# Two-layer hybrid encoder: the high and low parts of the 16 meta rows in one weight-load operand

## The chip, the cores and the metric

The kernel runs on one core of a Trainium2 chip. The metric is the device time of one execution, in microseconds (us). The trace is that of one profiled execution. Engines are called PE (TensorE, matrix products), PEld (TensorE's weight loads), DVE (VectorE), ACT (ScalarE), POOL (GpSimd) and SP (SyncE, which here only issues transfers).

## What is computed

The input has 512 rows of 1024 numbers, and 16 learned meta rows are put ahead of them. All is float32. Cut to what matters here:

```python
h = concat([meta, x])                                        # 528 x 1024
h = h + short_conv_mixer(rmsnorm(h, a_norm), a_w_in, a_conv, a_w_out)
h = h + hier_moe(rmsnorm(h, ffn_norm[0]), ...)               # 32 experts, top 2 of a group
kv = rmsnorm(h, kv_norm) @ w_kv                              # K and V, of all 528 rows
k = partial_rotary(k)
h = h[16:]                                                   # the meta rows end here
h = h + diff_attention(rmsnorm(h, b_norm), w_q, ..., k, v)   # q @ w_q of 512 rows
h = h + hier_moe(rmsnorm(h, ffn_norm[1]), ...)
return rmsnorm(h, final_norm)
```

## The kernel before

**Tiles.** The rows lie in five tiles: t = 0 to 3 with 128 rows of the input each, and t = NX = 4 with the 16 meta rows. The second layer (attention and its experts) has only the four full tiles.

**Products in high and low parts.** The dense products outside the experts run in fp32r. To keep float32's precision, each operand is split in two: ACT casts it to fp32r (the high part, `act_high`, `weight_high`), and DVE subtracts this from the original (the low part, `act_low`, `weight_low`). The helper `product` then makes, for each of the KC = 8 chunks of the contraction, three matmuls into one PSUM bank: high rows with high weights, high rows with low weights, low rows with high weights. The rows are the operand that is loaded as weights (128 columns for a full tile, 16 for the meta tile), and 512 columns of the weight matrix are what streams through. So a job, one tile by 512 output columns, is 24 matmuls, whether it has 128 rows or 16.

**Where the meta tile has jobs.** In the mixer's output projection of the first layer, `out_proj(0, 4)`: two jobs one after the other, the last of five tiles. And among the 28 JOBS of the K, V and Q projections, in this order: K columns 0 to 511 for tiles 0 to 4 (jobs 0 to 4), K columns 512 to 1023 (5 to 9), V in the same way (10 to 19), Q for tiles 0 to 3 (20 to 27). Jobs 4, 9, 14 and 19 are the meta tile's. In all, six jobs of 24 matmuls.

**Order of the work around the mixer's projection.** PE runs tile by tile: the projection of t, the transposes of tile t - 1 (`turn`, L873), the router's logits of tile t - 2 (L935). DVE adds the projection to the stream h (`add_tile`, L1303), ACT takes the root mean square and scales the row, PE transposes it. After the last tile DVE runs the routing, POOL gathers the first rows (L594), and the first expert starts. When PE has finished the last tile's projection it gives four units of the weight ring back (`pe.sem_inc(unit_used, 4)`); SP waits for that before it issues the first large burst of expert weights: six transfers of 2 MB.

**Order of the work in the projections.** PE runs job p into PSUM bank 4 + p % 4; it waits for ACT's copy of job p - 4 out of that bank. ACT copies job p, scaled with the row's factor, to `knat` (K and Q) or to `V` (L813), and then casts the quarter of the next weight unit that stands at p in SPLIT_AFTER. DVE applies the rotary embedding to job p (`rotate`, L1496 to L1499), copies the transposed heads of the job before (`take_rot`, L1507), and makes the low part of the quarter (L1222). PE transposes the rotated rows (`turn_rot`, L1115) one job late. After each meta job PE waits for its own matmuls and gives two ring units back, for which SP loads the next of w_kv, w_q or b_w_out.

**The experts.** Each expert takes three weight units of 2 MB from the ring or from the arena, SP reissues them as PE frees them, and POOL gathers the rows of each expert and scatters the results with indirect transfers.

## Time and profile before

| | us |
|---|---|
| runs of the kernel | 1638.17, 1640.92, 1640.74 |
| their median | 1640.74 |
| the profiled execution | 1639.19 |
| its span, first to last instruction | 1637.4 |
| mean granted TensorE clock | 0.940 of full speed |
| PE busy | 1362.4 (83%) |
| DVE busy | 382.0 (23%) |
| ACT busy | 315.6 (19%) |
| POOL busy | 189.9 (12%) |
| moved by the DMA engines | 472.66 MB |

The line names are those of the kernel before. Matmuls are pipelined and the end of each is modelled, so the duration of one (about 395 ns with 512 columns) is longer than the distance between the starts of two. A row of the timeline merges neighbouring instructions of a line: start, duration of the whole, engine, line, operation, what it writes and reads, how often, and in brackets the idle time of the engine ahead of it and what ended that. In the windows the clock is a share of 2.4 GHz: 1.00 and 0.50 are the two levels.

### The profile page before, as it was taken

The page shows a single profiled execution, that of the slowest core. Times are in us where ns is not written, and L with a number is a line of the kernel's source. Part 1 is how long each engine was busy: PE and PEld are TensorE (multiplying, and loading weights), DVE is VectorE, ACT ScalarE, POOL GpSimd, SP SyncE. Part 2 cuts the span into 40 slices and gives each one's busy share as a digit, 9 for nine tenths or more (in the row PEclk, how much of TensorE's full clock was granted, in tenths as well). Part 3 has the DMA queues.
Part 4 walks back from the last instruction along what each step waited for, and adds up shares of the span by engine and source line. Part 5 has one row for each costly group of instructions (what it writes and reads, how often), then busy time and mean ns, then how long its engine had stood idle before and what let it go on. Part 6 is the DMA issues. An engine that isn't in the chain of part 4 may idle for free. (4 is left out here: it accounts for less than half of the span.)

```text
span 1637.4 us, 17518 instructions
## 1 busy us (share of the span) xinstructions
PE 1362.4 (83%) x6689; PEld 757.7 (46%) x6689; DVE 382.0 (23%) x753; ACT 315.6 (19%) x601; POOL 189.9 (12%) x314
## 2 busy tenths in 40 slices
PE   5999994999888888775999978895999888888882
PEld 5999772333322322223676755783333322322320
DVE  3434423000000000004531388623000000000003
ACT  5222220101000000003322266431010000000002
POOL 2000001111111111111000000001112111111111
PEclk9999995999999999997999979996999999999996
DMA  9120417999999999994312110417999999999994
GB/s 344 41 104 1 167 60 315 417 425 426 425 426 427 426 425 426 425 417 168 127 52 103 52 52 1 154 55 305 415 425 427 425 426 427 424 424 425 426 377 162
DMA packets 60921, 472.66 MB, mean 289 GB/s; under 512 B 10592, under 2 KB 10668, under 8 KB 35776
## 3 DMA queue, kind: packets, MB, share of 16 engines
q1 hardware_dynamic: 46480, 441.48, 65.2%
q0 software_dynamic: 14384, 30.36, 5.0%
q8 instruction: 42, 0.69, 0.2%
q14 instruction: 15, 0.12, 0.0%
HBM read 465.17 MB, written 23.13 MB: 298 GB/s over the span
## 5 line engine op out<-in xcount | busy, mean ns | idle before, releaser
L947 PE MATMUL ps<-ring,act 128*64 128x512 f32 x1792 | 442.0, 646 | 76.4 <-DMA ring<-in_e_up 70.3
L947 PEld LDWEIGHTS ps<-ring,act 128*64 128x64 f32 x1792 | 139.8, 142 | 373.8 <-issue 373.8
L914 PE MATMUL ps<-parts 128*128 128x512 f32 (+1 forms) x1104 | 266.0, 399 | 8.3 <-DVE parts L1230 7.7
L970 PE MATMUL ps<-ring,act 128*64 128x512 f32 x896 | 204.6, 597 | 31.0 <-ACT act L767 31.0
L1413 DVE TENSOR_TENSOR act<-act,ps 128x256 f32<-128x256 f32 x64 | 26.9, 421 | 869.6 <-ACT act L765 869.6
L914 PEld LDWEIGHTS ps<-parts 128*128 128x128 f32 (+1 forms) x1104 | 194.7, 178 | 69.3 <-DVE parts L1230 5.9
L900 PE MATMUL ps<-parts 128*128 128x264 f32 x1152 | 144.5, 288 | 4.5 <-DVE parts L1224 2.9
L900 PEld LDWEIGHTS ps<-parts 128*128 128x128 f32 x1152 | 143.1, 191 | 5.5 <-issue 5.5
L765 ACT ACTIVATE act<-ps 128x256 f32<-128x256 f32 x64 | 24.5, 383 | 573.8 <-PE ps L947 573.8
L970 PEld LDWEIGHTS ps<-ring,act 128*64 128x64 f32 x896 | 70.8, 136 | 126.2 <-issue 126.2
L607 POOL COPY dst_now<-dst_row 128x1 uint32 (+1 forms) x64 | 11.6, 181 | 686.8 <-ACT act L774 686.8
L774 ACT COPY act<-ps 128x512 f32<-128x512 f32 x64 | 37.4, 585 | 247.2 <-PE ps L970 247.2
L594 POOL DMA_INDIRECT nat<-hn_rows,src_now x64 | 66.9, 1045 | 57.2 <-POOL src_now L591 54.5
L610 POOL DMA_INDIRECT expert_rows<-act,dst_now x64 | 65.4, 1022 | 58.3 <-POOL dst_now L607 54.8
L956 PEld LDWEIGHTS ps<-const,nat 128*128 128x128 f32 x256 | 36.2, 210 | 68.6 <-issue 68.6
L947 PE MATMUL ps<-arena,act 128*64 128x512 f32 x256 | 63.1, 645 | 1.8 <-DVE act L1407 1.8
L697 ACT CAST parts<-ring 128x1024 fp32r<-128x1024 f32 x40 | 41.3, 1047 | 106.9 <-PE ps L900 106.7
L956 PE MATMUL ps<-const,nat 128*128 128x128 f32 x256 | 48.7, 313 | 15.5 <-DMA nat<-hn_rows,src_now 15.5
L1224 DVE TENSOR_TENSOR parts<-ring,parts 128x1024 fp32r<-128x1024 f32 x40 | 48.3, 1222 | 55.9 <-ACT parts L697 55.8
L962 PE MATMUL ps<-const,act 128*128 128x128 f32 x128 | 30.5, 320 | 23.4 <-DVE act L1413 23.4
L1407 DVE TENSOR_TENSOR act<-ps,block_gain 128x512 f32<-128x512 f32 x64 | 43.7, 683 | 14.9 <-PE ps L956 14.9
L660 ACT ACTIVATE nat<-h 128x1024 f32<-128x1024 f32 (+1 forms) x23 | 24.3, 1055 | 109.6 <-DVE h L1303 90.7
(164 smaller groups left out, 915.8 us busy)
## 6 DMA issues: line engine op xcount, KB each, us to landing
ring<-in_e_gate SPq DMA_DIRECT2D x56, 2048.0 KB, 18.3
ring<-in_e_up SPq DMA_DIRECT2D x56, 2048.0 KB, 22.6
ring<-in_e_down SPq DMA_DIRECT2D x56, 2048.0 KB, 22.3
arena<-in_e_down SPq DMA_DIRECT2D x8, 2048.0 KB, 15.8
ring<-in_a_w_in SPq DMA_DIRECT2D x6, 2048.0 KB, 19.6
arena<-in_e_up SPq DMA_DIRECT2D x6, 2048.0 KB, 19.2
arena<-in_e_gate SPq DMA_DIRECT2D x6, 2048.0 KB, 14.2
ring<-in_w_kv SPq DMA_DIRECT2D x4, 2048.0 KB, 13.4
```

The lines of the kernel that those rows point to most:

```text
L594: pool.indirect_dma_start(nat[:, b, 0:DH], None, hn_halves[layer], bass.IndirectOffsetOnAxis(src_now[:, b:b + 1], 0), bounds_check=2 * (LE ...
L610: pool.indirect_dma_start(y_halves[layer], bass.IndirectOffsetOnAxis(dst_now[:, u:u + 1], 0), y_out[:, u, :], None, bounds_check=4 * SPREA ...
L697: last = nc.scalar.copy(high, src)
L774: nc.scalar.copy(y_out[:, u, :], ps[:, 6 + u, :]).then_inc(y_ready, 1)
L900: last = mm(ps[:, b + a, 0:HALF], w[:, k, :], acts[:, k, a * HALF:(a + 1) * HALF], start=(k == 0 and i == 0), stop=(k == KC - 1 and i == 2))
L914: last = mm(bank, x[:, k, :], w[:, k, :], start=(k == 0 and i == 0), stop=(k == KC - 1 and i == 2))
L947: last = mm(ps[f * C:(f + 1) * C, 2 + b, :].rearrange("p (g m i) -> p g m i", g=2, i=2), x, w, start=(k == 0), stop=(k == KC - 1))
L956: last = nc.tensor.transpose(ps[:, b, c * P:(c + 1) * P], nat[:, b, c:DH:KC // 2], ident)
L962: last = nc.tensor.transpose(ps[:, 4 + b, c * P:(c + 1) * P], hidden[:, b, c:FE // 2:2], ident)
L970: last = mm(ps[o * C:(o + 1) * C, 6 + b, :], hT[:, b, (2 * c + a) * C:(2 * c + a + 1) * C], w[:, f * D + o * DH:f * D + (o + 1) * DH], sta ...
L1224: last = v.tensor_tensor(low, src, high, ALU.subtract)
L1407: return v.tensor_tensor(xT[:, b, :].rearrange("p (c a n) -> p c a n", **shape), ps[:, b, :].rearrange("p (c a n) -> p c a n", **shape), b ...
```

## The change

A tile `packed` holds, for each of the 8 chunks, 48 columns: the high part of the 16 meta rows, the high part again, and the low part. ACT's cast writes both copies of the high part in one instruction (its source is broadcast), and DVE writes the low part to columns 32 to 47.

For a meta tile `meta_product` takes the place of `product`: per chunk one matmul with all 48 columns against the high weights, and one with the first 16 columns against the low weights. So 16 matmuls in place of 24. The wide one writes 48 PSUM partitions: 0 to 15 get high by high (and, accumulated, high by low from the narrow one), 16 to 31 get a copy that nobody reads, 32 to 47 get low by high.

What lies in partitions 32 to 47 has to be added, and DVE does it: in the mixer's projection with one `tensor_tensor` more ahead of the old one in `add_tile`, each over 16 x 1024; in the projections with `add_meta(p)` for the four meta jobs, a `scalar_tensor_tensor` over 16 x 512 from PSUM, scaled with the row's factor, onto what ACT has copied to `knat` or `V`. It waits for ACT's copy, stands ahead of `rotate(p)` on DVE, and DVE waits for its end. PE waits for it before job p + 4 uses the bank again, and before attention.

```diff
+LOW_AT = 32
+        packed = sb("packed", [P, KC, LOW_AT + META], F32R)
...
+        META_JOBS = [p for p, j in enumerate(JOBS) if j[2] == NX]
...
+            if t == NX and group in (1, 2):
+                high, low = packed[:, :, 0:META], packed[:, :, LOW_AT:]
...
+                if t == NX and group in (1, 2):
+                    src, high = bcast(src, 2, 2), packed[:, :, 0:LOW_AT].rearrange("p k (a n) -> p k a n", a=2)
                 nc.scalar.copy(high, src).then_inc(act_high_ready, 1)
...
+            def meta_product(bank, n):
+
+                w_low, w_high = (chunks(ring_parts[m % RING][:, :]) for m in (n, n + 1))
+                for k in range(KC):
+                    if k:
+                        mm(ps[0:META, bank, :], packed[:, k, 0:META], w_low[:, k, :], start=False, stop=False)
+                    last = mm(ps[0:LOW_AT + META, bank, :], packed[:, k, :], w_high[:, k, :], start=(k == 0), stop=(k == KC - 1))
+                    if not k:
+                        mm(ps[0:META, bank, :], packed[:, k, 0:META], w_low[:, k, :], start=False, stop=False)
+                return last
...
+                if p - 4 in META_JOBS:
+                    pe.wait_ge(meta_added, META_JOBS.index(p - 4) + 1)
...
             pe.wait_ge(proj_copied, len(JOBS))
+            pe.wait_ge(meta_added, len(META_JOBS))
...
                     dve.wait_ge(out_done, (NX + 1) * layer + t + 1)
+                    if t == NX:
+                        order(v.tensor_tensor(h[0:r, t, :], h[0:r, t, :], flat[LOW_AT:LOW_AT + r, b * W:(b + 2) * W], ALU.add))
                     v.tensor_tensor(h[0:r, t, :], h[0:r, t, :], flat[0:r, b * W:(b + 2) * W], ALU.add).then_inc(mixed, 1)
...
+            def add_meta(p):
+
+                kind, f, _ = JOBS[p]
+                dst = V[0:META, NX, f * W:(f + 1) * W] if kind == "v" else knat[0:META, ROT_JOBS.index(p) % 2, :]
+                dve.wait_ge(proj_copied, p + 1)
+                v.scalar_tensor_tensor(dst, ps[LOW_AT:LOW_AT + META, 4 + p % 4, :], rstd[0:META, NX:NX + 1], dst,
+                                       ALU.mult, ALU.add).then_inc(meta_added, 1)
+                dve.wait_ge(meta_added, META_JOBS.index(p) + 1)
+
             for p in range(len(JOBS)):
+                if p in META_JOBS:
+                    add_meta(p)
```

`out_proj` and `project` call `meta_product` where t == NX, and `product` as before elsewhere.

On PE, around the meta job 9 of the projections, the instructions of the kernel before stand in this order (the last number of a row is the columns that stream, the one before it the columns of the operand that is loaded):

```order
L1115 MATMUL ps<-const,knat 128x128 x3
L914 MATMUL ps<-parts 16x512 [waits proj_copied]
L914 MATMUL ps<-parts 16x512 x23
L1115 MATMUL ps<-const,knat 128x128 [waits proj_done,rot_copied,roped]
L1115 MATMUL ps<-const,knat 128x128 x3
```

And with the change, at the same place:

```order
L1135 MATMUL ps<-const,knat 128x128 x3
L920 MATMUL ps<-parts,packed 48x512 [waits proj_copied]
L922 MATMUL ps<-parts,packed 16x512
L919 MATMUL ps<-parts,packed 16x512
L920 MATMUL ps<-parts,packed 48x512
L919 MATMUL ps<-parts,packed 16x512
L920 MATMUL ps<-parts,packed 48x512
```

The rows go on in pairs of a narrow and a wide matmul, up to 8 of each; what stands ahead of the job and behind it is as it was.

On DVE, at the end of the mixer's projection of the first layer, the kernel before has the add of tile 3, the transposed tile 2, and then the meta tile's add:

```order
L1303 TENSOR_TENSOR h<-h,ps 128x1024 [waits out_done]
L1213 TENSOR_TENSOR act<-ps,gain 128x8x128 [waits turned1]
L1208 RECIPROCAL rstd<-ssq 128x1 [waits squared]
L1303 TENSOR_TENSOR h<-h,ps 16x1024 [waits out_done]
L1213 TENSOR_TENSOR act<-ps,gain 128x8x128 [waits turned1]
L1208 RECIPROCAL rstd<-ssq 16x1 [waits squared]
```

With the change:

```order
L1326 TENSOR_TENSOR h<-h,ps 128x1024 [waits out_done]
L1234 TENSOR_TENSOR act<-ps,gain 128x8x128 [waits turned1]
L1229 RECIPROCAL rstd<-ssq 128x1 [waits squared]
L1325 TENSOR_TENSOR h<-h,ps 16x1024 [waits out_done]
L1326 TENSOR_TENSOR h<-h,ps 16x1024 [waits dve_step]
L1234 TENSOR_TENSOR act<-ps,gain 128x8x128 [waits turned1]
```

Two adds in a row stand where one stood, the second behind a wait for the first.

On DVE in the projections, at job 4, the kernel before has:

```order
L1507 COPY arena<-ps 128x4x128 [waits rot_turned]
L1222 SCALAR_TENSOR_TENSOR parts<-ring,gain,parts 128x512 [waits w_high_ready]
L1222 SCALAR_TENSOR_TENSOR parts<-ring,gain,parts 128x512
L1496 TENSOR_TENSOR rope<-knat,const 16x128 [waits roped,proj_copied]
L1497 TENSOR_TENSOR rope<-knat,const 16x8x8 [waits dve_step]
```

With the change:

```order
L1530 COPY arena<-ps 128x4x128 [waits rot_turned]
L1243 SCALAR_TENSOR_TENSOR parts<-ring,gain,parts 128x512 [waits w_high_ready]
L1243 SCALAR_TENSOR_TENSOR parts<-ring,gain,parts 128x512
L1537 SCALAR_TENSOR_TENSOR knat<-ps,rstd,knat 16x512 [waits proj_copied]
L1519 TENSOR_TENSOR rope<-knat,const 16x128 [waits roped,proj_copied,meta_added]
```

The added row is `add_meta(4)`, ahead of the rotation of the meta rows.

## Rows read from the trace of the kernel before

**Rows 1.** The page, part 2: 40 slices of 40.9 us; granted clock and DMA, tenths.

```profile
PEclk9999995999999999997999979996999999999996
DMA  9120417999999999994312110417999999999994
```

**Rows 2.** Groups of instructions by form: busy us, mean ns, idle before.

```profile
L914 PE MATMUL ps<-parts 128*128 128x512 f32 x960 | 232.0, 400 | 8.3 <-DVE parts L1230 7.7 <-PE ps L914 0.6
...
L914 PE MATMUL ps<-parts 128*16 128x512 f32 x144 | 34.3, 395 | 0.0
```

**Rows 3.** Timeline, PE: first tiles of the mixer's projection; in the projections jobs 4, 11 to 14, 15 to 19.

```profile
177.09 25.09 PE L914 MATMUL ps<-parts 128*128 128x512 f32 x96 [3.20 <-DVE parts L1230]
...
798.18 0.66 PE L1115 MATMUL ps<-const,knat 128*128 128x128 f32 x4 [2.67 <-DVE knat L1499]
798.59 5.81 PE L914 MATMUL ps<-parts 128*16 128x512 f32 x24
...
841.79 22.50 PE L914 MATMUL ps<-parts 128*128 128x512 f32 x96
864.60 28.02 PE L914 MATMUL ps<-parts 128*128 128x512 f32 x120 [0.30 <-PE ps L914]
```

**Rows 4.** Timeline, ACT's copies of jobs 13 and 14.

```profile
858.78 0.69 ACT L813 ACTIVATE arena<-ps,rstd 128x512 f32<-128x512 f32 x1 [3.65 <-PE ps L914]
...
864.33 0.68 ACT L813 ACTIVATE arena<-ps,rstd 16x512 f32<-16x512 f32 x1 [3.64 <-PE ps L914]
```

**Rows 5.** Timeline, PE: mixer's projection of tiles 3 and 4, meta transposes, first expert's rows.

```profile
216.75 11.36 PE L914 MATMUL ps<-parts 128*128 128x512 f32 x48
...
230.62 11.29 PE L914 MATMUL ps<-parts 128*16 128x512 f32 x48
...
246.08 1.13 PE L873 MATMUL ps<-const,nat 16*128 16x16 f32 x8 [0.95 <-ACT nat L680]
...
275.47 1.10 PE L956 MATMUL ps<-const,nat 128*128 128x128 f32 x4 [9.32 <-DMA nat<-hn_rows,src_now]
```

**Rows 6.** Timeline, DVE: the meta tile's add in the mixer's projection.

```profile
241.95 1.21 DVE L1303 TENSOR_TENSOR h<-h,ps 16x1024 f32<-16x1024 f32 x1 [10.86 <-PE ps L914]
```

**Rows 7.** Timeline of SP's issues: the first of the weight burst, and w_q.

```profile
242.03 0.33 SPq L454 DMA_DIRECT2D arena<-in_e_gate  x1
...
835.15 29.81 SPq L427 DMA_DIRECT2D ring<-in_b_w_q  x2
```

**Rows 8.** Timeline, POOL: the first gather of each layer.

```profile
268.80 1.12 POOL L594 DMA_INDIRECT nat<-hn_rows,src_now  x1 [0.96 <-POOL src_now L591]
...
1129.22 1.12 POOL L594 DMA_INDIRECT nat<-hn_rows,src_now  x1 [0.93 <-POOL src_now L591]
```

**Rows 9.** Timeline, PE behind the second layer's first gather.

```profile
1132.61 1.10 PE L956 MATMUL ps<-const,nat 128*128 128x128 f32 x4 [6.19 <-DMA nat<-hn_rows,src_now]
```

**Rows 10.** Windows: length, busy PE, PEld, DVE, ACT, POOL, then clock, DMA share, GB/s.

```profile
273.00:274.00 1.00, 0.00 (x0) 0.00 (x0) 0.00 (x0) 0.00 (x0) 0.00 (x0) 0.50 0.82 312
...
1129.00:1130.00 1.00, 0.00 (x0) 0.00 (x0) 0.00 (x0) 0.00 (x0) 0.78 (x1) 0.50 0.68 279
```

**Rows 11.** Transfers of the whole run: count, KB each, median us from issue to landing.

```profile
ring<-in_b_w_q SPq DMA_DIRECT2D x2, 2048.0 KB, 8.7
...
nat<-hn_rows,src_now POOLq DMA_INDIRECT x64, 8.9
```

**Rows 12.** Timeline, DVE around the end of job 4.

```profile
801.61 1.41 DVE L1222 SCALAR_TENSOR_TENSOR parts<-ring,gain,parts 128x512 fp32r<-128x512 f32 x2
805.14 0.28 DVE L1496 TENSOR_TENSOR rope<-knat,const 16x128 f32<-16x128 f32 x1 [2.13 <-ACT knat L813]
...
806.16 0.67 DVE L1507 COPY arena<-ps 128x512 f32<-128x512 f32 x1
```

**Rows 13.** Windows (columns as in rows 10): a change of the clock, and the projections.

```profile
182.00:183.00 1.00, 1.00 (x4) 0.80 (x3) 0.71 (x1) 0.00 (x0) 0.00 (x0) 0.61 0.88 377
...
800.00:940.00 140.00, 138.48 (x621) 102.86 (x620) 45.12 (x105) 35.35 (x55) 0.00 (x0) 1.00 0.22 76
```

More of the change, by code:

```diff
@@ L276, in build @@
         combined = [sem(f"combined{l}") for l in range(2)]
-        proj_done, proj_copied = sem("proj_done"), sem("proj_copied")
+        proj_done, proj_copied, meta_added = sem("proj_done"), sem("proj_copied"), sem("meta_added")
         roped, rot_turned, rot_copied = sem("roped"), sem("rot_turned"), sem("rot_copied")
@@ L926, in out_proj @@
                 for f in range(2):
-                    last = product(ps[0:r, b + f, :], high, low, n + 2 * f, (S_AOUT, S_BOUT)[layer] + f * QUARTERS if t == 0 else None)
+                    last = meta_product(b + f, n + 2 * f) if t == NX else product(ps[0:r, b + f, :], high, low, n + 2 * f, (S_AOUT, S_BOUT)[layer] + f * QUARTERS if t == 0 else None)
                 last.then_inc(out_done, 1)
@@ L1100, in project @@
                 _, high, low = act_tile(T_KVQ + t)
-                last = product(ps[0:r, 4 + p % 4, :], high, low, U_KVQ + 2 * u, S_KVQ + u * QUARTERS if t == 0 else None)
+                last = meta_product(4 + p % 4, U_KVQ + 2 * u) if t == NX else product(ps[0:r, 4 + p % 4, :], high, low, U_KVQ + 2 * u, S_KVQ + u * QUARTERS if t == 0 else None)
                 last.then_inc(proj_done, 1)
```

## The prediction

> **What bounds the kernel now.** Begin with the slices [rows 1]. In slices 8 to 18 and again in most of 28 to 38 the DMA engines are at 9 tenths: there the experts' weights stream, and the time of these stages is bytes over bandwidth, whatever PE does. The change touches neither; it can only move their start. What it touches lies in slice 5 (the mixer's projection of the first layer) and in slices 19 to 22 (the K, V and Q projections), where DMA is at 0 to 4 tenths. So the questions are whether PE sets the pace in these two places, and what stands behind each.
>
> The groups by form give the size [rows 2]: 144 matmuls with 16 loaded columns, 34.3 us busy, with no idle time ahead of them. Their mean of 395 ns is not what one costs, since neighbours overlap. The cost is the distance of starts. Jobs 15 to 19 are 120 matmuls in 28.02 us [rows 3]: (28.02 - 0.395) / 119 = 0.232 us each. One of these five jobs is the meta tile's. Alone, ACT's copies of jobs 13 and 14 follow each other by 5.55 us, which is the meta job 14: 5.55 / 24 = 0.231 us [rows 4]. In the mixer the meta tile's 48 take 11.29 us, the 128 rows' 48 take 11.36 us [rows 5]: (11.29 - 0.395) / 47 = 0.232. So a matmul costs 0.232 us with 16 and with 128 loaded columns alike, and a wide one of 48, which lies between, is priced at 0.232 too.
>
> In the projections PE is the pace: from 800 to 940 us it is busy for 138.48 of 140 us [rows 13], and its longest wait in the stage's jobs is the 2.67 us ahead of job 4, for DVE's rotation [rows 3]. In the mixer's projection PE runs from tile to tile as well; the meta tile is last, and DVE (10.86 us idle) waits for it [rows 6].
>
> **Part 1, the matmuls of the projections.** Four meta jobs lose 8 matmuls each: 32 x 0.232 = 7.4 us, all on PE's path. A new thing is the alternation of 48 and 16 columns, 64 times in these jobs, which no row shows. A border from 128 to 16 columns without anything between is that of jobs 13 and 14, and it shows in neither distance [rows 4]. For a bound from the other side take job 4 by itself, (5.81 - 0.395) / 23 = 0.235 us [rows 3]: 0.003 us more, over 96 matmuls in both stages 0.3 us. I take nothing, and see no reason for a gain.
>
> The Trainium skill, "TensorE: Matmul & The Clock Gate", section "Back-to-back issue gap", gives about 216 ns between matmuls of 512 columns at the full clock, and 131 ns in a sustained stream of weight loads and matmuls. By these the 48 removed matmuls would be worth 10.4 or 6.3 us instead of 11.1. The trace has 232 ns in just this stream, and the sum goes by the trace.
>
> **Part 2, what comes due earlier in the projections.** Every meta job ends 1.86 us sooner. What must be ready then?
> DVE, at job 4: the low part of the fourth quarter of the next weights ends at 803.02 [rows 12]. Job 5 would start at about 802.85 + 0.4, and needs that quarter only for its last two chunks, 18 x 0.232 = 4.2 us later. The first job after each meta job is covered by some 4 us.
> `add_meta(4)`: no row has this instruction. Its neighbours are one 512 column low part (half of 1.41, 0.70 us), a copy from PSUM (0.67 us) [rows 12], and half of the 16 x 1024 add (0.61 us) [rows 6]; I take 0.7, between 0.6 and 0.75. It starts when ACT's copy is there, near 803.3, and ends at 804.0; the rotation (1.0 us, from 805.14 to 806.16 in [rows 12]) ends at 805.0. PE asks for it behind job 5, near 808.9. Cover 3.8 us. What queues behind it on DVE is the rotation and the copy of the heads; before, DVE stood idle for 2.13 us there [rows 12], and the 1.86 us of job 4 and the 0.7 us use it up nearly. At jobs 14 and 19 there is no rotation, and only the add.
> PE's new wait at jobs 8, 13, 18 and 23 looks at an add four jobs old: nothing.
> ACT's cast writes 256 numbers a partition in place of 128; by its copy of 512 in 0.68 us [rows 4] that is at most 0.2 us. In the mixer it runs under tile 3's 11.36 us [rows 5]; ahead of job 4 it is in the stretch where ACT and DVE prepare jobs, so at most 0.2 us could reach the path. I take 0.
> SP: ring units come back earlier, so transfers shift with the jobs. For w_q the issue is at 835.15 [rows 7] and it takes 8.7 us [rows 11]; its first quarter is cast behind job 15, after 864.33 + 5.5 us. Over 20 us of cover.
> Projections: 7.4 us, from 7.1 to 7.5.
>
> **Part 3, the mixer's projection.** PE ends the meta tile 16 x 0.232 = 3.71 us sooner, at 238.2. Two things hang on this end.
> First, SP's weight burst: its first issue stands at 242.03 [rows 7], right behind PE. It moves by the full 3.71 us.
> Second, the chain to the router: DVE now adds twice. The new add is like the old, 1.21 us [rows 6], and one waits for the other, by estimate 0.03 us: 1.24 us. ACT, PE's meta transposes (246.08, rows 5), the logits, the routing on DVE and the gather on POOL move by 3.71 - 1.24 = 2.47 us.
> Both meet in the first gather. POOL issues it at 268.80 [rows 8], and PE starts on it at 275.47 [rows 5]: 6.6 us. In the second layer it took from 1129.22 to 1132.61 [rows 8, 9], 3.4 us. The difference is the burst. In the first layer the DMA engines are busy until about 273.9 (the window from 273 has 0.82), 5.1 us into the gather; in the second they are just running dry (0.68 at 1129) [rows 10]. Under full load a gather takes 8.9 us in the median [rows 11]. So under load it goes ahead at 3.4 / 8.9 = 0.38 of its free pace: 5.1 x 0.38 = 1.9 us of its work is done when the burst ends, 1.5 remain, 275.4. This fits the trace. It then moves with 0.62 of the burst's shift and 0.38 of its own: 0.62 x 3.71 + 0.38 x 2.47 = 3.2 us.
> Bounds: if the gather simply came behind the burst, 3.7 us; if only its issue counted, 2.5 us; if it were as free as in the second layer, it would land at 266.3 + 3.4 = 269.7, 5.6 us sooner. I take 3.2.
>
> The Trainium skill, "DMA: Bandwidth & Descriptors", section "Queues, rings and completion order", says that each DMA engine takes turns between the queues that have work. That speaks for the shared pace and against the strict "behind the burst": by it 3.2 us, by the other 3.7 us.
>
> The experts' stage then starts 3.2 us sooner and keeps its length, since its weights stream at full bandwidth from the first release on; its end and everything after moves along.
>
> **The sum.** 3.2 + 7.4 = 10.6 us. Against the profiled execution, 1639.19 - 10.6 = 1628.6. The median of the runs before is 1.55 us above the profiled execution, and the mean of the four executions is 1639.8; from it the time is 1629.2, which I give. About 3.3 us, 0.2%, is what a measurement can tell from no change.
>
> **Rivals.**
> The projections' gain is filled up again: the shorter meta jobs uncover DVE, as ahead of job 4 already (2.67 us). For it: 0.7 us more on DVE at each. Against it: the covers of 3.8 to 4 us. If all four lose their 1.86 us, 3.2 us remain: 1636.6.
> The mixer's gain is lost: PE's first expert starts as before, from something in the routing that I don't see. 7.4 us remain: 1632.4. For it only that the gather's landing is modelled.
> The gather is freed altogether: 5.6 + 7.4 = 13.0, 1626.8. Against it: the burst is still running for 3.9 us of it.
> The change doesn't do what it says: a matmul that writes 48 partitions costs as much as two of 16. Then 16 cost what 24 did, and the added add is left: +1.24 x 0.38 = 0.5 us, 1640.3. Against it: 128 columns cost 0.232 us.
> Slower: the granted clock. Its price is in the first 96 matmuls of the mixer's projection: 25.09 us where 96 take 22.50 later [rows 3], and the clock stands at the low level until within the window from 182 [rows 13], 5.4 us: PE loses half of the time spent at the low level. The place would be the projections: if fewer busy columns, 16 or 48 in the meta jobs, and PE's waits let the clock fall to 1.2 GHz, more than 10.6 / 0.5 = 21 us at the low level turn the gain into a loss. From job 4 to job 11 are 43 us [rows 3]; run low they would cost 21.6: 1629.2 + 21.6 = 1650.8. Against it: from 800 to 940 the clock is at 1.00 through all four meta jobs [rows 13], which were narrower then.
>
> **Chances.** Forecast 0.80, with a range of its own from 1626 to 1632; mixer's gain lost 0.05; gather freed 0.05; projections filled up 0.04; no effect 0.03; clock 0.03. The unknown costs make the gain 9.4 to 13.0 us, and single executions differ by about 1.4 us to each side. The range from 1625.0 to 1633.5 takes in the first three cases. Faster by over 0.2%: 0.80 + 0.05 + 0.05 + 0.03 of the filled case = 0.93. Within 0.2%: 0.04. Slower: 0.03.
>
> **What would show each step.** In the profile after: 96 matmuls for six meta jobs, copies of ACT around job 14 apart by 16 x 0.232 = 3.7 us. The burst's first issue near 238.3; DVE's two adds of 1.2 us; the first gather issued near 266.3 and PE on it near 272.2. Job 0 of the projections 3.2 us earlier, attention 10.6 us earlier, both experts' stages as long as before, and no wait of PE on DVE behind jobs 5 and 10. Copies of 5 us or more around job 14 would make part 1 wrong; PE at 273.0 with the gather issued at 266.3 the model of the gather; a clock of 0.50 between 800 and 930 the case of the clock.

## The result, and the profile after

| | before | after |
|---|---|---|
| median | 1639.45 us (1637.59 to 1640.92, 4 runs) | 1625.8 us (1624.37 to 1629.28, 4 runs) |
| profiled execution | 1639.19 us | 1626.44 us, span 1624.7 us |
| matmuls on PE | 6689 | 6641 |
| DVE instructions | 753 | 758 |

The ratio is 0.9915, interval 0.9898 to 0.9931: 13.7 us less, where 10.6 were forecast. 1629.2 us was given with a range from 1625.0 to 1633.5. The time lies in the range, 3.4 us under the forecast. The experiments below put the change itself at about 11 us, and the other 2.6 us at differences between executions of the same kernel.

The page of the kernel after, its slices of the granted clock and of the DMA engines, to be held against [rows 1]:

```profile
PEclk9999995999999999997999979996999999999996
DMA  9130427999999999995312200427999999999984
```

The experts' stages are again full of DMA, and no slice of the clock stands lower than before. The changes are too small for a slice and must be looked for in the timeline.

The groups of PE's matmuls by form (out<-in, tile, count, busy us, mean ns, idle before), against [rows 2]:

```profile
L932 PE MATMUL ps<-parts 128*128 128x512 f32 x960 | 231.4, 399 | 8.3 <-DVE parts L1251 7.7 <-PE ps L920 0.6
L920 PE MATMUL ps<-parts,packed 128*48 128x512 f32 x48 | 19.5, 409 | 0.0
```

The 144 narrow matmuls have become 48 wide ones (128*48) and 48 narrow ones. The wide one's mean of 409 ns against 395 of the old narrow one is no price: busy times of neighbours overlap, and some of these matmuls ran at the low clock (below).

The timeline of PE in the mixer's projection, against [rows 3, 5]: first 96 matmuls, the first wide one of the meta tile, the meta transposes, the first expert's rows.

```profile
176.18 24.04 PE L932 MATMUL ps<-parts 128*128 128x512 f32 x96 [3.20 <-DVE parts L1251]
...
228.64 0.41 PE L920 MATMUL ps<-parts,packed 128*48 128x512 f32 x1
...
241.63 1.14 PE L880 MATMUL ps<-const,nat 16*128 16x16 f32 x8 [2.20 <-ACT nat L685]
...
269.90 1.10 PE L974 MATMUL ps<-const,nat 128*128 128x128 f32 x4 [7.77 <-DMA nat<-hn_rows,src_now]
```

The same stretch on DVE, SP and POOL, against [rows 6 to 8]:

```profile
236.25 1.21 DVE L1325 TENSOR_TENSOR h<-h,ps 16x1024 f32<-16x1024 f32 x1 [7.14 <-PE ps L920]
237.50 1.21 DVE L1326 TENSOR_TENSOR h<-h,ps 16x1024 f32<-16x1024 f32 x1
```

```profile
236.34 0.33 SPq L459 DMA_DIRECT2D arena<-in_e_gate  x1
```

```profile
264.78 1.12 POOL L599 DMA_INDIRECT nat<-hn_rows,src_now  x1 [0.95 <-POOL src_now L596]
```

These have to be read against a zero point. The projection already starts 0.91 us sooner, and its first 96 matmuls take 24.04 us instead of 25.09, with the same instructions. The matmuls behind them start at 202.90 before and at 200.92 after: 1.98 us that lie ahead of everything the change touches. Taking them off:

| event | before | after | difference | less 1.98 | forecast |
|---|---|---|---|---|---|
| first issue of the weight burst | 242.03 | 236.34 | 5.69 | 3.71 | 3.71 |
| meta transposes | 246.08 | 241.63 | 4.45 | 2.47 | 2.47 |
| first gather issued | 268.80 | 264.78 | 4.02 | 2.04 | 2.47 |
| PE on the gathered rows | 275.47 | 269.90 | 5.57 | 3.59 | 3.2 |

The two adds of DVE take 1.21 us each and start 1.25 us apart (1.24 forecast), and the transposes move exactly as forecast. The gather is *issued* 0.43 us less early than forecast: the logits took 4.70 us instead of 4.29, since the granted clock fell to 0.50 as they began (in the window from 242, they start at 242.70), and before it fell within them (in the window from 247, they start at 247.14). And yet PE starts 0.4 us *earlier* than the model of the gather gave. This is the first thing to be settled.

In the projections, PE at job 3, ahead of job 4, ahead of job 5 and in it, and the 96 matmuls behind job 14, against [rows 3]:

```profile
782.73 5.82 PE L932 MATMUL ps<-parts 128*128 128x512 f32 x24
...
792.14 1.12 PE L1135 MATMUL ps<-const,knat 128*128 128x128 f32 x4 [2.56 <-DVE knat L1522]
...
798.22 0.63 PE L1135 MATMUL ps<-const,knat 128*128 128x128 f32 x4 [0.30 <-PE ps L920]
798.60 5.81 PE L932 MATMUL ps<-parts 128*128 128x512 f32 x24
...
854.35 22.48 PE L932 MATMUL ps<-parts 128*128 128x512 f32 x96 [0.30 <-PE ps L920]
```

ACT's copies of jobs 13 and 14, against [rows 4]:

```profile
850.39 0.69 ACT L820 ACTIVATE arena<-ps,rstd 128x512 f32<-128x512 f32 x1 [3.65 <-PE ps L932]
...
854.08 0.68 ACT L820 ACTIVATE arena<-ps,rstd 16x512 f32<-16x512 f32 x1 [1.78 <-PE ps L920]
```

The copies lie 3.69 us apart instead of 5.55, so job 14 lost 1.86 us: 8 x 0.232, as forecast. Job 9 lost 1.87 and job 19 lost 1.83. Behind jobs 4, 9 and 14 PE waits for nothing but its own last matmul (0.30 us). But at job 4 it is less. From job 3's start to job 5's are 15.87 us (782.73 to 798.60), and before it is 16.31 us, from these two rows of PE before:

```profile
788.77 5.82 PE L914 MATMUL ps<-parts 128*128 128x512 f32 x24
...
805.08 5.81 PE L914 MATMUL ps<-parts 128*128 128x512 f32 x24
```

That is 0.44 us less where 1.86 were forecast. The windows of the kernel after (columns as in [rows 10]) say why:

```profile
791.00:792.00 1.00, 0.00 (x0) 0.00 (x0) 0.90 (x6) 1.00 (x2) 0.00 (x0) 0.89 0.00 0
792.00:793.00 1.00, 0.86 (x5) 0.87 (x5) 1.00 (x3) 0.77 (x2) 0.00 (x0) 0.50 0.00 0
793.00:794.00 1.00, 1.00 (x5) 0.42 (x4) 1.00 (x3) 0.00 (x0) 0.00 (x0) 0.50 0.00 0
...
795.00:796.00 1.00, 1.00 (x5) 0.42 (x4) 1.00 (x3) 0.00 (x0) 0.00 (x0) 0.90 0.00 0
```

PE had stood idle for 2.56 us ahead of this job, waiting for the rotation on DVE, and the granted clock went from 1.00 to 0.50 (from 2.4 to 1.2 GHz) there and came back within the window from 795. The matmuls in it start 0.43 us apart instead of 0.232. Three microseconds at half speed are the 1.42 us that are missing. That is the mechanism of the rival "the granted clock", in small. Is it the change's doing? This is the second thing.

The third is the size of the whole: 13.7 us in the medians, 12.75 in the two traces, and not 10.6. At the end of the projections the two traces stand 12.07 us apart. Of it 5.57 are there at the first expert's rows (1.98 of them ahead of the change) and 5.56 at jobs 9, 14 and 19, 0.44 at job 4; the rest, some 0.5 us, are small differences of both signs between the stages. From there through attention to the end of its output projection both take 161.18 us.

### The profile page after: what moved, and what is told of

It is laid out like the page before. It is cut to its first block and busy times, and to the rows that moved or that the text cites. A ratio compares the mean times of both kernels' runs of the same rounds, so it can differ in the third digit from the quotient of the medians.

```text
span 1624.7 us, 17432 instructions
## 1 busy us (share of the span) xinstructions
PE 1348.6 (83%) x6641; PEld 753.7 (46%) x6641; DVE 386.4 (24%) x758; ACT 315.6 (19%) x601; POOL 190.3 (12%) x314
## 5 line engine op out<-in xcount | busy, mean ns | idle before, releaser
L932 PE MATMUL ps<-parts 128*128 128x512 f32 x960 | 231.4, 399 | 8.3 <-DVE parts L1251 7.7
L932 PEld LDWEIGHTS ps<-parts 128*128 128x128 f32 x960 | 180.8, 190 | 50.4 <-DVE parts L1251 5.9
L907 PEld LDWEIGHTS ps<-parts 128*128 128x128 f32 x1152 | 142.2, 190 | 5.5 <-issue 5.5
L974 PE MATMUL ps<-const,nat 128*128 128x128 f32 x256 | 48.7, 314 | 13.7 <-DMA nat<-hn_rows,src_now 13.7
## 6 DMA issues: line engine op xcount, KB each, us to landing
ring<-in_e_down SPq DMA_DIRECT2D x56, 2048.0 KB, 22.5
```

The lines of the kernel that those rows point to most:

```text
L907: last = mm(ps[:, b + a, 0:HALF], w[:, k, :], acts[:, k, a * HALF:(a + 1) * HALF], start=(k == 0 and i == 0), stop=(k == KC - 1 and i == 2))
L932: last = mm(bank, x[:, k, :], w[:, k, :], start=(k == 0 and i == 0), stop=(k == KC - 1 and i == 2))
L974: last = nc.tensor.transpose(ps[:, b, c * P:(c + 1) * P], nat[:, b, c:DH:KC // 2], ident)
```

## Experiments 1: each half alone, and the matmuls put back

Theory: 7.4 us come from four meta jobs of the projections and 3.2 to 3.7 from the mixer's meta tile, and both come from the 8 matmuls of 24 that a job loses. The rival says that something else in the change (the packed operand, the other order of operands, shifted transfers) brings a part.

The changed kernel again, as the base of this series, unaltered.

> The changed kernel once more, for a second trace and a tighter interval. Sum of the parts (32 matmuls of 0.232 us in the projections, 3.2 to 3.7 us through the mixer): 10.6 to 11.1 us less than the kernel before, ratio 0.9933. Rival, that something beyond these parts is systematic: the first comparison's 13.7 us again, ratio 0.9915. In the trace: 6 meta jobs of 16 matmuls, each 1.86 us shorter; the stretch up to the mixer's projection as in the kernel before but for the moment at which the clock rises.

The packed operand only in the mixer (group 1); the projections as before, without `add_meta`:

```
-            if t == NX and group in (1, 2):
+            if t == NX and group == 1:
                 high, low = packed[:, :, 0:META], packed[:, :, LOW_AT:]
...
-                last = meta_product(4 + p % 4, U_KVQ + 2 * u) if t == NX else product(
+                last = product(
...
-        META_JOBS = [p for p, j in enumerate(JOBS) if j[2] == NX]
+        META_JOBS = []
```

> Only the mixer's projection of the meta tile uses the packed operand (32 matmuls in place of 48, two adds on DVE); the projections of K and V have 24 matmuls a meta job and no add_meta. The sum of the parts: 3.2 us less than before if the gather shares the DMA engines with the weight burst, 3.7 us if it lands behind the burst's end; ratio 0.9979. Rival, that more comes from this place (gather freed as in the second layer): 5.6 us, ratio 0.9966.

Only in the projections (group 2); the mixer as before:

```
-            if t == NX and group in (1, 2):
+            if t == NX and group == 2:
...
-                    last = meta_product(b + f, n + 2 * f) if t == NX else product(
+                    last = product(
...
-                    if t == NX:
-                        order(v.tensor_tensor(h[0:r, t, :], h[0:r, t, :], flat[LOW_AT:LOW_AT + r, b * W:(b + 2) * W], ALU.add))
```

> Only the four meta jobs of the K and V projections use the packed operand; the mixer's projection is as before. All on PE's path: 32 x 0.232 = 7.4 us less, ratio 0.9955, at most 1.1 us of it lost where the clock is low in job 4. Rival, that DVE's added 0.74 us per job fills the gap: PE waits on DVE behind jobs 5 and 10, 0 to 3 us less.

Everything as in the changed kernel, but each narrow matmul issued twice, so that a job has 24 again:

```
-                    if k:
+                    for _ in range(2 if k else 0):
                         mm(ps[0:META, bank, :], packed[:, k, 0:META], w_low[:, k, :], start=False, stop=False)
...
-                    if not k:
+                    for _ in range(0 if k else 2):
```

> The changed kernel with its packed operand, its adds and its waits, but each chunk of a meta job has one narrow matmul more (high by low is made and counted twice, so this part of the meta rows' sum is wrong), 24 matmuls a job as before. If the gain is PE's matmuls alone, nothing is left of it: the added adds cost 1.24 us ahead of the router and are covered in the projections, 0 to 1.2 us more than before, ratio 1.0000 to 1.0008. Rival, that part of the gain comes from elsewhere (other operand, other placement of tiles, shorter weight loads): 2 to 3 us less than before, ratio 0.9985.

Measured, in five rounds beside the kernel before (median 1639.52 us, 1635.0 to 1643.6, 23 runs):

| kernel | median (range, runs) | ratio to before | gain |
|---|---|---|---|
| changed, again | 1629.74 (1626.55 to 1630.67, 6) | 0.9933 [0.9919, 0.9948] | 11.0 us |
| mixer only | 1635.66 (1631.35 to 1640.03, 12) | 0.9973 [0.9962, 0.9984] | 4.4 us |
| projections only | 1632.9 (1631.38 to 1636.17, 6) | 0.9954 [0.9938, 0.9970] | 7.5 us |
| 24 matmuls again | 1638.36 (1634.88 to 1643.21, 12) | 0.9992 [0.9979, 1.0006] | 1.3 us |

Three things follow. The gain is that of the removed matmuls: with them put back, at 48 and 16 columns, what remains is a ratio of 0.9992. Its interval takes in 1, but also the 0.9985 of the rival by which 2 to 3 us come from elsewhere, so the time alone does not settle it. The trace does, in the projections. ACT's copies of jobs 13 and 14 in this kernel:

```profile
862.22 0.69 ACT L820 ACTIVATE arena<-ps,rstd 128x512 f32<-128x512 f32 x1 [3.65 <-PE ps L932]
867.78 0.68 ACT L820 ACTIVATE arena<-ps,rstd 16x512 f32<-16x512 f32 x1 [3.65 <-PE ps L920]
```

They are 5.56 us apart, as in the kernel before (5.55), where 16 matmuls have 3.69. So the number of matmuls carries it, and the alternation of wide and narrow ones costs 0.01 us in a job. The two parts are 7.5 and 4.4 us; with the ratio's interval the first stands within 4.9 to 10.2 us and the second within 2.6 to 6.2. Both agree with 7.4 and with 3.2 or 3.7 for the mixer, and can't tell these two apart. And the changed kernel itself gains 11.0 us in this series, not 13.7; the two intervals overlap.

The kernel with the doubled matmuls shows what 16 of them cost in the path of the mixer's end: its burst is issued at 242.71 and PE is on the first rows at 275.81, where the changed kernel of the same series has 236.49 and 270.10. Its first 96 matmuls end 2.48 us later (202.84 and 200.36); this taken off, the burst moves by 3.74 us, 16 x 0.232 = 3.71, and the rows by 3.2.

## Experiments 2: does the first gather go by its issue, or by the burst?

The prediction let the gather go ahead at 0.38 of its free pace under the burst's load, so that it moves with 0.62 of the burst's shift and 0.38 of its own. The rival: its rows land behind the burst, however early it is issued. Two kernels pull the two apart.

The burst later: SP waits until DVE has added the meta tile; the chain to the gather is left as it is.

```
                 sp.wait_ge(unit_used, U_MOE[layer])
+                if layer == 0:
+                    sp.wait_ge(mixed, NX + 1)
```

> The changed kernel, but SP waits for DVE's last add of the mixer's projection before it issues the first layer's weight burst, 2.45 us later than PE's end. POOL's gather is issued as before. Behind the burst: PE's first expert starts 33.5 us after the burst's first issue as in the six traces so far, so 2.45 us later against PE's end than in the changed kernel, and the gather takes 7.6 us. Shared pace: 0.62 of 2.45, 1.5 us later. Issue alone: no difference.

The gather's issue earlier: the added add of the low part is left out.

```
-                    if t == NX:
-                        order(v.tensor_tensor(h[0:r, t, :], h[0:r, t, :], flat[LOW_AT:LOW_AT + r, b * W:(b + 2) * W], ALU.add))
```

> The changed kernel without the added add on DVE in the mixer's projection (the low part of the meta rows is not added to the stream in the first layer). The chain to the router is 1.24 us shorter, and the gather is issued that much sooner. Behind the burst: PE's first expert starts no sooner, 33.5 us after the burst's first issue, the gather takes 6.4 us. Shared pace: 0.5 us sooner. Issue alone: 1.24 us sooner.

The first kernel took 1633.56 us and the second 1630.31, in a single execution each. Such a time can't tell a microsecond. What counts is the distances inside each trace. SP's first issue, POOL's gather and PE's first rows, burst later:

```profile
241.10 0.33 SPq L459 DMA_DIRECT2D arena<-in_e_gate  x1
```

```profile
267.07 1.12 POOL L601 DMA_INDIRECT nat<-hn_rows,src_now  x1 [0.95 <-POOL src_now L598]
```

```profile
274.31 1.10 PE L976 MATMUL ps<-const,nat 128*128 128x128 f32 x4 [9.89 <-DMA nat<-hn_rows,src_now]
```

And one add only, POOL and PE (its burst is issued at 238.18):

```profile
264.67 1.12 POOL L599 DMA_INDIRECT nat<-hn_rows,src_now  x1 [0.95 <-POOL src_now L596]
```

```profile
272.17 1.10 PE L974 MATMUL ps<-const,nat 128*128 128x128 f32 x4 [10.14 <-DMA nat<-hn_rows,src_now]
```

All traces side by side but the two with an earlier burst, which follow below. E is the end of the first 96 matmuls of the mixer's projection, B the burst's first issue, G the gather's, S PE's start on its rows. The last two rows belong to the third series, below:

| kernel | G - B | S - G | S - B | S - E |
|---|---|---|---|---|
| before | 26.77 | 6.67 | 33.44 | 73.29 |
| before, again | 27.19 | 6.14 | 33.33 | 73.17 |
| projections only | 26.59 | 6.58 | 33.17 | 73.02 |
| changed | 28.44 | 5.12 | 33.56 | 69.68 |
| changed, again (first series) | 28.43 | 5.18 | 33.61 | 69.74 |
| mixer only | 28.44 | 5.46 | 33.90 | 70.03 |
| 24 matmuls again | 28.44 | 4.66 | 33.10 | 72.97 |
| burst later | 25.97 | 7.24 | 33.21 | 71.80 |
| one add only | 26.49 | 7.50 | 33.99 | 70.11 |
| changed, again (third series) | 28.44 | 5.20 | 33.64 | 69.77 |
| job 4 ahead | 28.42 | 5.17 | 33.59 | 69.72 |

G - B varies by 2.47 us, from 25.97 to 28.44. By the shared pace S - B should vary with it. The five short ones (before twice, projections only, burst later, one add only) have a mean G - B of 26.60 us, the six others of 28.44; 0.38 of the difference is 0.70 us. Instead their means of S - B, 33.43 and 33.57, differ by 0.14 us, with a scatter of 0.3 to 0.6 us to each side. A straight line through the eleven points has a slope of 0.07, with a 95% interval from -0.14 to 0.28: neither the 0.38 of the shared pace nor the 1 of "only its issue" lies in it. The time from the gather's issue, S - G, is what gives, from 4.66 to 7.50 us.

The two kernels made for this question, counted from E, against 69.7 in four traces of the changed kernel's mixer: with the burst 2.47 us later S comes 2.1 later, where "behind the burst" asks for 2.5, the shared pace for 1.5 and "only its issue" for nothing. With one add the gather is issued 1.95 us sooner (1.2 of it the add, the rest logits that ran at the upper clock), and S comes 0.4 us later, where the three ask for 0, 0.7 sooner and 1.95 sooner. So the rival fits best: in the first layer the rows are there some 33.5 us behind the burst's first issue, and the gather's own issue counts for little or nothing. The scatter of some half a microsecond that none of the models gives is not traced, and a share of the issue below 0.28 is not excluded.

The kernel before was run once more in this series, to see how much of the differences lies in the execution.

> The kernel before, for a second trace of it. Two readings of the clock ahead of job 4 of the projections, where PE stands idle for 2.6 us: in four of four traces of the changed kernel and its variants, and in the variant that has the old projections too, it fell to the low level there, in the first trace of the kernel before it did not. If the fall is a matter of the execution, it is as likely to fall here too. If it comes with the change, it doesn't fall. The gather: behind the burst, PE's first expert 33.5 us after the burst's first issue.

It took 1642.17 us, span 1640.3. In the mixer the first 96 matmuls took 22.52 us where [rows 3] have 25.09, and its burst was issued at 238.95 and not at 242.03 [rows 7]: 3.1 us sooner, and still its span was 2.9 us longer in the whole. So single places of one kernel differ by 2 to 3 us from execution to execution, as much as the 1.98 us that had to be taken off above. In this place it is the granted clock. The same 96 matmuls in this trace and in that of the changed kernel of the third series:

```profile
176.59 22.52 PE L914 MATMUL ps<-parts 128*128 128x512 f32 x96 [3.20 <-DVE parts L1230]
```

```profile
177.29 25.33 PE L932 MATMUL ps<-parts 128*128 128x512 f32 x96 [3.20 <-DVE parts L1251]
```

In each of the thirteen traces PE waits 3.20 us ahead of them. In two (this one and the early burst's, below) the clock stayed at 1.00 and they took 22.5 us; in five it fell and was back by the window from 181, 23.8 to 24.1 us; in six it was back only in the windows from 182 or 183, 25.1 to 25.4 us. The changed kernel is in both of the latter groups. So 1.05 of the 1.98 us above are a shorter fall of the clock, and not the change. The other 0.91 lie in the start of the 96 matmuls, which in three traces of the changed kernel itself stands at 176.18, 176.30 and 177.29. At job 4 the trace of before, again, shows this, PE:

```profile
796.64 1.12 PE L1115 MATMUL ps<-const,knat 128*128 128x128 f32 x4 [2.66 <-DVE knat L1499]
797.40 6.85 PE L914 MATMUL ps<-parts 128*16 128x512 f32 x24
```

The idle time of 2.66 us is as long as in [rows 3] (2.67), but the old job of 24 takes 6.85 us where it took 5.81: here the clock fell in the kernel before too. Of the traces with this idle time (2.55 to 2.67 us) it did not fall in the first one of before and in "one add only", and it fell in the nine others. It fell within the wait or up to 1.5 us behind it. How long it stayed at the low level differs: some 3 us in the changed kernel's first trace, nearly 7 in the second.

What this costs can be read from job 3's start to job 5's. Five of the traces:

| kernel | clock | job 3 to job 5 |
|---|---|---|
| before | stays up | 16.31 |
| before, again | low for some 3 us | 17.72 |
| one add only (job 4 as in the changed kernel) | stays up | 14.45 |
| changed | low for some 3 us | 15.87 |
| changed, again (first series) | low for nearly 7 us | 17.25 |

At the upper level in both, the change is worth 16.31 - 14.45 = 1.86 us at job 4 too, exactly 8 x 0.232. A fall costs 1.4 us in either kernel, the long one 2.8. So the fall goes with the wait ahead of job 4, which both kernels have, and it came with the old job of 24 matmuls too.

## Experiments 3: the burst earlier, and the wait ahead of job 4 taken away

Both findings name something that can be had. If the gather lands behind the burst, the burst should begin sooner. Ring slots of the first half of the last tile's weights are free once its half f = 0 is multiplied, and the first two transfers of the burst can go there. This stands in both layers. For it the last matmul of that half signals `half_done`, two loads wait on it instead of on the last unit, and DVE adds the two halves apart:

```
-        out_done = sem("out_done")
+        out_done, half_done = sem("out_done"), sem("half_done")
...
+                    if f == 0 and t == (NX if layer == 0 else NX - 1):
+                        last.then_inc(half_done, 1)
...
+                load(1, 0, "down", "half")
+                load(2, 1, "gate", "half")
                 sp.wait_ge(unit_used, U_MOE[layer])
...
-                load(1, 0, "down", None)
-                for part in ORDER:
+                for part in ORDER[1:]:
                     load(2, 1, part, None)
```

> The changed kernel with two additions: SP issues the two transfers whose ring units the first half of the last tile's projection frees already behind that half (1.86 us sooner in the first layer, 5.6 us in the second), and DVE adds each half of the last tile on its own, so that only the second half's adds stand behind PE's end (1.2 us less). Behind the burst: first expert 1.9 us sooner in the first layer, and by the shorter add 0.6 us in the second, 2.5 us less than the changed kernel, ratio to the kernel before 0.9918. Rival, that the burst isn't what the gather waits for: 1.2 us in the first layer and 0.6 in the second, ratio 0.9922; or that the transfers which the experts need first now come later: 0 or slower than the changed kernel.

It was timed in the second series, five rounds: 1625.88 us (1623.07 to 1626.58, 5 runs) beside 1639.39 of before, ratio 0.9910 [0.9895, 0.9926]. SP, POOL and PE:

```profile
231.64 0.33 SPq L459 DMA_DIRECT2D ring<-in_e_down  x1
```

```profile
262.87 1.12 POOL L603 DMA_INDIRECT nat<-hn_rows,src_now  x1 [0.95 <-POOL src_now L600]
```

```profile
266.00 1.10 PE L980 MATMUL ps<-const,nat 128*128 128x128 f32 x4 [5.79 <-DMA nat<-hn_rows,src_now]
```

The halved adds let the gather go out sooner as well, at 262.87. Now it takes 3.13 us, where the second layer of before has 3.4 [rows 8, 9]: that is a gather that the burst no longer holds up. The first issue came 3.77 us sooner, counted from the end of the first 96 matmuls, and not the 1.86 us of the expectation, since half of the meta tile is a whole job of 16 matmuls. S - B is 34.36 here, above all others, and S - E is 66.71, 3.0 us under the changed kernel. PE seems to wait for the gather alone, so a still earlier burst should bring nothing; this was not run. The 0.6 us expected in the second layer don't show: from the issue of `in_e_gate` into the arena, behind PE's last matmul, to PE's first rows are 30.47 us, and 30.02 to 30.55 in the changed kernel's three traces.

The other one: at job 4 DVE's rotation of job 2 is late. The transposes of that rotation are now put behind job 4 on PE, and job 4 ahead of them:

```
-                while p >= NX - 1 and nrot < len(ROT_JOBS) and ROT_JOBS[nrot] <= p - 1:
+                while p >= NX - 1 and nrot < len(ROT_JOBS) and ROT_JOBS[nrot] <= p - (2 if p == NX - 1 else 1):
```

> The changed kernel, but PE runs job 4 of the projections before the transposes of job 2's rotated rows, for which it has waited 2.6 us in all ten traces so far, and in eight of them the clock fell to the low level there and stayed for 3 to 7 us. Clock as a matter of PE's idle time: no idle, no fall, 2.6 us less idle (some of it may come back as a wait for job 3's rotation or the weights of job 5) and 1 to 3 us less at the low clock: 2 to 4 us less than the changed kernel, ratio to the kernel before 0.991 to 0.993 where the changed kernel has 0.9933. Rival, that DVE's chain of rotations is the bound and not PE's order: the wait comes back in full ahead of job 5, nothing gained but the clock.

Both edits together:

> Both additions in one kernel: early burst and halved adds (their run gave ratio 0.9910), and job 4 first. If they act in different stages and don't meet, the gains add: 2 to 4 us under the early burst's, ratio 0.989 to 0.990. Rival, that the early burst's gain was the spread of executions: 0.991 to 0.992.

And the changed kernel once more beside them:

> The changed kernel a third time, on the chip of the two before, for the comparison with them: ratio 0.9933 as in its second comparison, 10.6 to 11.1 us less than the kernel before. If the first comparison's 0.9915 was more than spread, this one lies below 0.9925.

Measured in five rounds beside the kernel before (1642.37 us, 1637.83 to 1644.24, 11 runs):

| kernel | median (range, runs) | ratio to before | gain |
|---|---|---|---|
| changed, again | 1630.92 (1627.96 to 1632.33, 6) | 0.9932 [0.9915, 0.9949] | 11.2 us |
| job 4 ahead | 1623.7 (1621.94 to 1627.21, 6) | 0.9895 [0.9877, 0.9912] | 17.2 us |
| job 4 ahead, burst earlier | 1621.95 (1620.6 to 1623.52, 4) | 0.9884 [0.9864, 0.9903] | 19.1 us |

PE in the kernel with job 4 ahead:

```profile
782.91 5.82 PE L932 MATMUL ps<-parts 128*128 128x512 f32 x24
...
793.76 0.63 PE L1135 MATMUL ps<-const,knat 128*128 128x128 f32 x4 [0.30 <-PE ps L920]
795.28 0.66 PE L1135 MATMUL ps<-const,knat 128*128 128x128 f32 x4 [0.89 <-DVE knat L1522]
795.69 5.81 PE L932 MATMUL ps<-parts 128*128 128x512 f32 x24
```

From job 3's start to job 5's are 12.78 us (782.91 to 795.69). In the changed kernel's trace shown above, job 3 starts at 782.73 and job 5 at 798.60: 15.87 us. So 3.1 us are gone: 1.67 of idle time (2.56 to 0.89), and the clock's 1.4, since it stays at its upper level throughout. Against the long fall it would be 4.5. The fastest kernel, with both edits, has 12.79 us there, and no fall either. With the wait of 2.6 us the clock stayed up in two traces of eleven, so two of two without it speak for the wait as the cause, but are few.

The measured difference of the third series is 7.2 us of medians (1630.92 to 1623.7), more than the 2 to 4 us that were expected and the 3.1 to 4.5 that the traces give. Of the 6.6 us between the two spans (1628.6 and 1622.0), 3.0 are at job 4, and 2.4 are already there at the burst's first issue (238.75 and 236.38), ahead of anything that differs in these kernels; 1.27 of them are the longer fall of the clock in the first 96 matmuls (25.33 and 24.06 us). So here too a part is the execution's; the 3 us at job 4 are the edit's.

The earlier burst's kernel gained 14.7 us in its series where the changed one had 11.0 and 11.2 in the others, with overlapping intervals, and 1.8 us on top of the other edit, again with overlap: its 3.0 us at the first rows are seen in the trace, its worth in the whole is not settled. Both together are the fastest that was run, and their interval [0.9864, 0.9903] lies clear of the changed kernel's, [0.9915, 0.9949].

## Why the prediction was right, and where it was not

**Part 1, 0.232 us per matmul: right.** Jobs 9, 14 and 19 lost 1.87, 1.86 and 1.83 us against 8 x 0.232 = 1.86. Projections alone gave 7.5 us against 7.4, and in the kernel with 24 matmuls the job had its old 5.56 us again. The step that carried it was to take the distance of starts and not the mean duration, and to see that 16 and 128 loaded columns have the same distance, so that 48 must too. Of the Trainium skill's two figures for this, 216 and 131 ns ("TensorE: Matmul & The Clock Gate", "Back-to-back issue gap"), the first would, as an estimate, have put the gain at 10.4 us, which the second and third comparison can't tell from 11; the second, an estimate of 6.3 us, lies outside the changed kernel's interval in all three series. The distances in the traces, 3.69 us for 16 matmuls, bear out the 0.232.

The alternation was taken at 0 with a bound of 0.3 us: right. Its weight load of 48 columns takes longer than one of 16, but is hidden under the matmul before it, and the copies around job 14 are 3.69 us apart, 16 matmuls of 0.231. The groups of weight loads of the changed kernel:

```profile
L920 PEld LDWEIGHTS ps<-parts,packed 128*48 128x48 f32 x48 | 6.1, 127 | 6.3 <-issue 0.6
L919 PEld LDWEIGHTS ps<-parts,packed 128*16 128x16 f32 x42 | 4.1, 97 | 5.1 <-issue 0.7
```

**Part 2, the covers: right for jobs 9, 14 and 19, right for DVE at job 4, incomplete for PE there.** `add_meta` was put at 0.7 us, and takes 0.74:

```profile
798.66 0.74 DVE L1537 SCALAR_TENSOR_TENSOR knat<-ps,rstd,knat 16x512 f32<-16x512 f32 x1 [1.69 <-ACT knat L820]
```

PE did not wait for DVE behind jobs 5 and 10. What was missed is the clock. The prediction had this mechanism as its rival for a slower kernel, gave it the right price (half of the time at the low level) and spoke against it on one trace in which the clock happened not to fall. It asked for 21 us at the low level. The runs showed 3 to 7, in most executions, of the kernel before as well; so it costs 1.4 or 2.8 us of either and moves the ratio by chance only. A wait that stands in both kernels was passed over as belonging to neither. Where the clock fell it cost 3.1 to 4.5 us, about as much as the mixer's part of the change brought.

**Part 3, the mixer: right in what moves, with one term from a wrong model.** The burst's 3.71 us, the added add's 1.21 us and the chain's 2.47 us as far as the meta transposes are met to a few hundredths; the gather's issue moved by 2.04, since the clock took 0.41 us in the logits, a thing that the chain left out. The step that failed is the gather's pace: "0.62 x 3.71 + 0.38 x 2.47 = 3.2 us". In its place stands the burst, whose shift is 3.7 us. The size of the term was less wrong than its model: the trace of after has 3.59, and counted from E five traces with the changed mixer (69.68 to 70.03) stand 3.4 us under three with the old one (73.02 to 73.29), between the two. The prediction had the burst's whole shift as a bound, "if the gather simply came behind the burst", and chose the other by one fit: 6.6 us under the burst and 3.4 without explain each other with a pace of 0.38, but this pace was itself made from the median of gathers in another stage (8.9 us in [rows 11]). One point can't separate a pace from a queue; the kernels with G - B changed did. The Trainium skill says that each DMA engine takes turns between queues that have work ("DMA: Bandwidth & Descriptors", section "Queues, rings and completion order"). The prediction read from this that an earlier gather lands earlier, and the runs don't bear this reading out: the one with its add removed, which was issued 26.49 us behind its burst instead of 28.44, took 7.50 us instead of 5.12. They do not show *why* it stays behind, whether in the engines' queues or at the memory. In the rival of the freed gather, "5.6 us sooner" should be 275.47 - 269.7 = 5.8 us, which makes its time 1626.6 and not 1626.8.

PE on the first rows, forecast near 272.2, came at 269.90: 1.98 us of this lie ahead of the change, 0.4 are the gather's term.

**The sum.** By the burst it is 7.4 + 3.7 = 11.1 us, by the traces' mean for the mixer 10.8, against gains of 11.0 and 11.2 in the second and third comparison; their intervals reach some 2.5 us to each side and exclude neither of them, nor the forecast's 10.6. The first one gave 13.7. Of its 2.6 us more, 1.98 can be pointed at in the two traces, ahead of the changed code, and 1.05 of these are the clock's; the rest is not traced to one place. They are differences between executions: the same kernel before ran from 1635.0 to 1644.24 us over all series. The median of 1625.8 us lies 0.2 us below the 1626 to 1632 that the prediction gave to its own case, and nearer to the 1626.8 of the freed gather than to 1629.2: the wide range held by the spread of executions, and what decides for the forecast's case is the traces. The size was estimated 0.2 to 0.5 us too low, and the first measurement showed 2.6 too much.

**The rivals.** No effect (a wide matmul costs two): fell, by the copies 3.69 us apart. Slower by the clock: fell; in the projections it was low for 3 to 7 us at one wait, not for 21. Mixer's gain lost: fell, 4.4 us with an interval clear of zero. Projections filled up: fell, 7.5 us. Gather freed altogether: not in this change, S - G stayed at 5.1 us; but the kernel with the earlier burst freed it, and had 3.13 us.

## What to carry to other kernels

Price a matmul in a stream by the distance of starts, from two rows with different shapes, and then count instructions: where 16 rows cost what 128 cost, operands that share the streamed side belong side by side in one weight load. Where two things compete for DMA, one trace gives one point; before choosing between "shared" and "behind", look for a second point with another offset, or keep the whole distance between the bounds as the term's range. And look at the waits that stand in both kernels: a wait of 2.6 us of PE ahead of a long run of matmuls, harmless in the one trace at hand, cost 3.1 to 4.5 us where the clock fell, about what the mixer's part of this change brought.

## What the runs showed of the hardware

The rows of the first layer's first gather were in use on PE 33.1 to 34.0 us behind the first issue of a weight burst in eleven traces, whether it had been issued 25.97 or 28.44 us behind it; freed of the burst it took 3.1 us.

After 2.55 to 2.67 us of idle time on PE the granted clock fell to 0.50 in nine of eleven traces, also of the kernel before, and stayed there for some 3 to 7 us; with an idle time of 0.89 and 0.90 us in its place it did not fall, in two of two.

Around an idle time of 3.20 us on PE ahead of another stage it fell in eleven of thirteen traces; the stage's first 96 matmuls took 22.5 us without a fall and 23.8 to 25.4 with one.

A matmul of 512 columns with a weight load ahead of it kept its distance of 0.23 us with 16, 48 and 128 loaded columns and in alternation of 48 and 16, while the loads themselves took 97, 127 and 190 ns on the mean.
